# Norm factors by a full matrix of ones in seven root-mean-square norms of a two-stack transformer kernel

## The chip, the cores and the metric

The kernel runs on one core of one Trainium2 chip. The metric is the device time of one execution in microseconds (us), the median of several runs. The engines are named as the profile names them: PE (TensorE matmul), PEld (its weight loads), DVE (VectorE), ACT (ScalarE), POOL (GpSimd), SP (the queue that issues the DMAs).

## The reference

Two stacks of two layers each over 512 positions (and 256 context positions in the first layer) with 1024 channels: attention and a Fourier mix, gated linear attention and mLSTM style mixers, sliding attention, and feed-forward blocks. What matters here is the norm that stands ahead of nearly every block:

```python
def rms_norm(x, g):
    xf = x.astype(jnp.float32)
    y = xf * lax.rsqrt(jnp.mean(xf * xf, axis=-1, keepdims=True) + NORM_EPS)
    return (y * g.astype(jnp.float32)).astype(x.dtype)
```

The mean runs over the 1024 channels of one position, and one factor per position then scales all its channels.

## The kernel before, in words

Activations lie transposed: channels on the 128 partitions, positions along the free axis, so that x is KT = 8 tiles of 128 x n, with n = 768 (512 positions and 256 of context) in the first layer and n = 512 later. Every projection is `linear` (L393 is its matmul line): PE takes a unit of 128 x 1024 weights, split by ACT (L340, WHI) and DVE (L349, WLO) into two parts, and does three passes of each tile against a high and a low part of the activations. Those two parts are made by the norm ahead of the projection.

A norm needs sums over partitions. Class `Squares` gathers them: as each output tile of the projection before it is ready, ACT squares it (`square`, L533), tile 0 straight into RS and the others into one of two SQ buffers, and DVE adds tiles 1 to 6 to RS (`add`, L543). The last tile, 7, stays in SQ. Then `root` (L622) runs the steps below, each waiting for the one before it:

- PE, `Squares.sums` (L545 to L558): for each piece t of 128 positions, a matmul with 128 columns of RS as the stationary side and one column of ones as the moving side (L553), and the same for SQ (L556); the sums of 128 positions come out as one column of 128 partitions in bank 7. That is n/128 pairs: 4, or 6 for n = 768.
- ACT: square root of these 4 or 6 columns, into RC (L652); the mean's scale and the epsilon go in as scale and bias.
- DVE: reciprocal of 4 or 6 columns (L662).
- PE: spread (L640): one matmul per 128 positions with the broadcast column as stationary side and the identity as moving side, so that bank 6 (and 7 for n = 768) holds the factor of each position on every partition.
- DVE then scales: `normalize` (L700), `final_norm` (L2739) or `add_normed` (L2783), one `scalar_tensor_tensor` per tile, x times gain times the factor, which it reads from PSUM (`root_of`, L666). ACT makes the high part (L691, L689, L2808), DVE the low part (L715, L713, L2791), and PE starts the next `linear` when tile 0 of both is there. In the norms with a modulation, DVE makes the gains of both conditions between the reciprocal and the first scaling (`prep`, L731, two small operations).

While these steps run, no other work is queued on PE, so that it stands still outside L553, L556 and L640. `Squares` with this `root` is used in seven norms, here numbered by their place: norm 1 (first stack, layer 0, ahead of the feed-forward, n = 768), norm 2 (layer 1, ahead of the mixer, n = 768), norm 3 (layer 1, ahead of the feed-forward), norm 4 (`final_norm` of the first stack), norm 5 (second stack, `add_normed` behind the first mixer), norm 6 (`normalize` ahead of the second mixer), norm 7 (`add_normed` behind the second mixer), the last five with n = 512. Four other calls of `root` don't take the changed way: two use `LateSquares` (sums by PE tile by tile, L585), and two carry a `mean` (L649, L659). `TileNorm` (L974 to L996) has its own copy of the old steps.

The order of all work is the order of the code on each engine; ring buffers and semaphores (`mark`, `wait_ge`) tie the engines together.

Of the kernel before, what the change touches and what calls it, by code (L numbers as in the profile page):

```python
# [512 lines left out]
class Squares:  # L513


    def __init__(self, c, nk, n, size):
        self.c, self.nk, self.n, self.size = c, nk, n, size
        self.squared = c.mark("act", nk)
        self.added = c.mark("dve", nk - 2)
        self.summed = c.mark("pe")  # L520

    def place(self, k):
        return self.c.sq(k, self.n) if k else self.c.RS[:, 0:self.n]
# [21 lines left out]
    def sums(self, pe):  # L545

        c = self.c
        for token in c.bank_free.get(7, ()):
            pe.wait_ge(*token)
        pe.wait_ge(*self.added.at(self.nk - 2))  # L550
        for t in range(self.n // P):
            out = c.bank(7, 1, NC + t)
            pe.matmul(out, c.RS[:, t * P:(t + 1) * P], c.ONES[:, 0:1], start=True, stop=False)  # L553
            if t == 0:
                pe.wait_ge(*self.squared.at(self.nk))
            mm = pe.matmul(out, self.place(self.nk - 1)[:, t * P:(t + 1) * P], c.ONES[:, 0:1], start=False, stop=True)  # L556
        mm.then_inc(*self.summed.up())
        return self.summed.at(1)  # L558


class LateSquares:


    def __init__(self, c, nk, n, size):
        self.c, self.nk, self.n, self.size = c, nk, n, size
        self.squared = c.mark("act", nk)
        self.added = c.mark("pe", nk)
        self.given = 0

    def square(self, act, k, source, ready, bias=None):  # L570
        act.wait_ge(*ready)
# [50 lines left out]
def root(c, squares, over, mean=None):  # L622


    sqrt, rec, spread = c.mark("act"), c.mark("dve"), c.mark("pe")
    floored = c.mark("dve") if mean is not None else None
    n = squares.n
    nt = n // P
    summed = []
    block = c.stage()  # L630

    @block.tensor
    def _(pe):
        summed.append(squares.sums(pe))
        for token in c.bank_free.get(6, ()):
            pe.wait_ge(*token)
        pe.wait_ge(*rec.at(1))
        for t in range(nt):
            out = c.bank(6, P, t * P) if t < 4 else c.bank(7, P, (t - 4) * P)
            mm = pe.matmul(out, c.RC[:, 8 + t:9 + t].broadcast_to([P, P]), c.ID[:], start=True, stop=True)  # L640
        mm.then_inc(*spread.up())
        c.bank_free[6] = [over]
        c.bank_free[7] = [over] if nt > 4 else [sqrt.at(1)]

    @block.scalar
    def _(act):
        if mean is not None:
            act.wait_ge(*floored.at(1))
            act.activation(c.RC[:, 0:nt], c.RC[:, 0:nt], ACT.Sqrt).then_inc(*sqrt.up())  # L649
            return  # L650
        act.wait_ge(*summed[0])
        act.activation(c.RC[:, 0:nt], c.bank(7, nt, NC), ACT.Sqrt, bias=c.EPSC[:, 0:1], scale=1.0 / squares.size).then_inc(*sqrt.up())  # L652

    @block.vector
    def _(dve):
        if mean is not None:
            dve.wait_ge(*mean.taken.at(2))
            dve.wait_ge(*summed[0])
            dve.scalar_tensor_tensor(c.RC[:, 0:nt], c.bank(7, nt, NC), 1.0 / squares.size, c.RC[:, 4:4 + nt], ALU.mult,  # L659
                                     ALU.add).then_inc(*floored.up())  # L660
        dve.wait_ge(*sqrt.at(1))
        dve.reciprocal(c.RC[:, 8:8 + nt], c.RC[:, 0:nt]).then_inc(*rec.up())  # L662
    return spread


def root_of(c, lo, n):  # L666

    return c.bank(6, n) if lo == 0 else c.bank(7, n)


def normalize(c, squares, gain, xp, shift=None, keep=None, prep=None):


    n, nk = squares.n, squares.nk
    parts = conds(n)
    scaled, hi, lo = c.mark("dve", nk), c.mark("act", nk), c.mark("dve", nk)
    xh, xl, xw = xp
    spread = root(c, squares, scaled.at(nk))
    block = c.stage()
    place = keep or (lambda k, a, m: c.ht(k % 3, a, m))  # L680

    @block.scalar
    def _(act):
        for k in range(nk):
            act.wait_ge(*scaled.at(k + 1))
            for q, a, m in parts:
                o = xh[:, k * xw + a:k * xw + a + m]
                if shift is None:
                    ins = act.activation(o, place(k, a, m), ACT.Copy)  # L689
                else:  # L690
                    ins = act.activation(o, place(k, a, m), ACT.Identity, bias=shift(k, q))  # L691
            ins.then_inc(*hi.up())

    @block.vector
    def _(dve):
        def scale(k):
            if k >= 3:
                dve.wait_ge(*lo.at(k - 2))
            for q, a, m in parts:
                ins = dve.scalar_tensor_tensor(place(k, a, m), c.x(k, a, m), gain(k, q), root_of(c, a, m), ALU.mult, ALU.mult)  # L700
            ins.then_inc(*scaled.up())
        if prep is not None:
            prep(dve)
        dve.wait_ge(*spread.at(1))
        scale(0)
        for k in range(nk):
            if k + 1 < nk:
                scale(k + 1)
            dve.wait_ge(*hi.at(k + 1))
            for q, a, m in parts:  # L710
                o = slice(k * xw + a, k * xw + a + m)
                if shift is None:
                    ins = dve.tensor_tensor(xl[:, o], place(k, a, m), xh[:, o].bitcast(F32), ALU.subtract)  # L713
                else:
                    ins = dve.scalar_tensor_tensor(xl[:, o], place(k, a, m), shift(k, q), xh[:, o].bitcast(F32), ALU.add, ALU.subtract)  # L715
            ins.then_inc(*lo.up())
    return lambda k: lo.at(k + 1)
# [231 lines left out]
class TileNorm:  # L949
# [50 lines left out]
    def apply(self, dve):  # L1000
        dve.wait_ge(*self.spread.at(1))
        for k in range(self.nk):
            for q, a, m in conds(self.n):
                x = self.tiles_of[k](a, m)
                ins = dve.scalar_tensor_tensor(x, x, self.gain(k), root_of(self.c, a, m), ALU.mult, ALU.mult)
            ins.then_inc(*self.done.up())


# [1718 lines left out]
def final_norm(c, squares, late):  # L2727


    scaled = c.mark("dve", KT)  # L2730
    spread = root(c, squares, scaled.at(KT))
    block = c.stage()
    out = lambda k: c.H[:, k * NL:(k + 1) * NL]

    @block.vector
    def _(dve):
        dve.wait_ge(*spread.at(1))
        for k in range(KT):
            dve.scalar_tensor_tensor(out(k), c.x(k), c.vec("g_final", k), root_of(c, 0, NL), ALU.mult, ALU.mult).then_inc(*scaled.up())  # L2739

    @block.scalar
    def _(act):
        for k in range(KT):
            late.square(act, k, out(k), scaled.at(k + 1))
    c.X, c.H, c.stride = c.H, c.X, NL
    return scaled.at(KT)
# [24 lines left out]
def add_normed(c, squares, gain, dst, xp, mean=None, up=None):  # L2771


    scaled, added = c.mark("dve", KT), c.mark("dve", KT)
    hi, lo = c.mark("act", KT), c.mark("dve", KT)
    spread = root(c, squares, scaled.at(KT), mean)
    block = c.stage()
    xh, xl, xw = xp

    @block.vector  # L2780
    def _(dve):
        def scale(k):
            dve.scalar_tensor_tensor(dst(k), dst(k), c.vec(gain, k), root_of(c, 0, NL), ALU.mult, ALU.mult).then_inc(*scaled.up())  # L2783

        def low(k):
            dve.wait_ge(*hi.at(k + 1))
            q = slice(k * xw, k * xw + NL)
            if up is None:
                ins = dve.tensor_tensor(xl[:, q], c.x(k), xh[:, q].bitcast(F32), ALU.subtract)
            else:  # L2790
                ins = dve.scalar_tensor_tensor(xl[:, q], c.x(k), c.vec(up, k), xh[:, q].bitcast(F32), ALU.mult, ALU.subtract)  # L2791
            ins.then_inc(*lo.up())
        dve.wait_ge(*spread.at(1))
        scale(0)
        for k in range(KT):
            if k + 1 < KT:
                scale(k + 1)
            dve.wait_ge(*scaled.at(k + 1))
            dve.tensor_tensor(c.x(k), c.x(k), dst(k), ALU.add).then_inc(*added.up())  # L2799
            if k:  # L2800
                low(k - 1)
        low(KT - 1)

    @block.scalar
    def _(act):
        for k in range(KT):
            act.wait_ge(*added.at(k + 1))
            act.activation(xh[:, k * xw:k * xw + NL], c.x(k), ACT.Copy,  # L2808
                           scale=1.0 if up is None else c.vec(up, k)).then_inc(*hi.up())
    return lambda k: lo.at(k + 1)  # L2810
# [268 lines left out]
```

## Time and profile before

| | |
|---|---|
| median of 3 runs | 3479.46 us (3477.65 to 3481.04) |
| profiled execution, its own time | 3470.54 us |
| its span, first to last instruction | 3468.8 us |
| mean granted TensorE clock | 0.957 of full |
| PE busy | 3229.4 us, 93% |
| PEld busy | 2542.6 us, 73% |
| DVE busy | 1550.0 us, 45% |
| ACT busy | 1167.3 us, 34% |
| POOL busy | 193.2 us, 6% |
| `linear` matmuls, L393 | 2049.6 us (x7200) and 1245.7 us (x3600) |

Busy times are those of the profiled execution, and shares are of its span. The granted clock is the share of full speed (2.4 GHz) that PE was given; 0.50 is 1.2 GHz. Matmuls are pipelined, and their ends are modelled. The f32 matmuls of a norm stand in the trace as two records each ("x16" are eight matmuls). The number in brackets behind a timeline row is how long the engine sat idle before it, and what ended that.

### The profile page before, as it was taken

The page shows a single profiled execution, that of the slowest core. Times are in us where ns is not written, and L with a number is a line of the kernel's source. Part 1 is how long each engine was busy: PE and PEld are TensorE (multiplying, and loading weights), DVE is VectorE, ACT ScalarE, POOL GpSimd, SP SyncE. Part 2 cuts the span into 40 slices and gives each one's busy share as a digit, 9 for nine tenths or more (in the row PEclk, how much of TensorE's full clock was granted, in tenths as well). Part 3 has the DMA queues.
Part 4 walks back from the last instruction along what each step waited for, and adds up shares of the span by engine and source line. Part 5 has one row for each costly group of instructions (what it writes and reads, how often), then busy time and mean ns, then how long its engine had stood idle before and what let it go on. Part 6 is the DMA issues. An engine that isn't in the chain of part 4 may idle for free.

```text
span 3468.8 us, 42192 instructions
## 1 busy us (share of the span) xinstructions
PE 3229.4 (93%) x17354; PEld 2542.6 (73%) x17354; DVE 1550.0 (45%) x2331; ACT 1167.3 (34%) x1892; POOL 193.2 (6%) x222
## 2 busy tenths in 40 slices
PE   7898899999999899999998899999999887899998
PEld 5655587887888656778887677878888665688886
DVE  2145535434445345464555453254444455354444
ACT  3134433313223234343334532233223333332232
POOL 0012200000000012100000010000000024100000
PEclk9899999999999899999998899899999888899998
DMA  6500013333112200122222101122222110122221
GB/s 242 211 18 1 1 49 143 112 117 139 61 61 90 82 10 1 49 85 97 97 91 72 53 32 43 37 79 103 93 96 97 59 49 25 67 98 92 97 97 55
DMA packets 74030, 269.26 MB, mean 78 GB/s; under 512 B 9064, under 2 KB 9832, under 8 KB 72560
## 3 DMA queue, kind: packets, MB, share of 16 engines
q1 hardware_dynamic: 73840, 266.57, 21.8%
q8 instruction: 139, 2.28, 0.3%
q14 instruction: 51, 0.42, 0.0%
HBM read 264.44 MB, written 2.10 MB: 77 GB/s over the span
## 4 chain that ended last, share of the span: by engine, by line
PE 83%; DVE 8%; ACT 3%; issue 3%; DMA 2%; POOL 1%; SPq 0%; POOLq 0%; ACTq 0%; DVEq 0%
PE PS L393 62%; PE PS L1285 2%; PE PS L1262 2%; PE PS L1188 2%; PE PS L480 2%; DVE room L1468 1%; PE PS L1272 1%; POOL room L2582 1%; PE PS L585 1%; PE PS L1242 1%; DMA RING<-in_stream 1%; PE PS L640 1%; DMA room<-in_w_ada 1%; PE PS L2905 1%; DVE H L2799 1%
## 5 line engine op out<-in xcount | busy, mean ns | idle before, releaser
L393 PE MATMUL PS<-room,WHI 128*128 128x512 f32 (+1 forms) x7200 | 2049.6, 381 | 54.9 <-DVE room L715 13.8
L393 PEld LDWEIGHTS PS<-room,WHI 128*128 128x128 f32 x7200 | 1275.7, 191 | 353.6 <-issue 98.8
L393 PE MATMUL PS<-room,WLO 128*128 128x512 f32 (+1 forms) x3600 | 1245.7, 376 | 0.0
L393 PEld LDWEIGHTS PS<-room,WLO 128*128 128x128 f32 x3600 | 640.5, 191 | 128.8
L349 DVE TENSOR_TENSOR WLO<-RING,WHI 128x1024 fp32r<-128x1024 f32 x371 | 453.6, 1223 | 383.9 <-ACT WHI L340 382.9
L340 ACT ACTIVATE WHI<-RING 128x1024 fp32r<-128x1024 f32 x371 | 390.1, 1054 | 545.7 <-PE PS L393 534.4
L831 DVE SCALAR_TENSOR_TENSOR H<-PS,VEC,H 128x511 f32<-128x511 f32 (+1 forms) x132 | 83.1, 657 | 307.4 <-ACT H L809 307.4
L809 ACT ACTIVATE H<-PS,VEC 128x512 f32<-128x512 f32 (+1 forms) x132 | 88.4, 703 | 349.0 <-PE PS L393 349.0
L1262 PE MATMUL PS<-room 96*128 96x256 f32 (+1 forms) x432 | 154.3, 476 | 11.2 <-ACT SQ L1373 7.7
L774 DVE SCALAR_TENSOR_TENSOR X<-PS,MOD,X 128x512 f32<-128x512 f32 x96 | 60.5, 658 | 221.4 <-PE PS L393 221.3
L1468 DVE TENSOR_REDUCE room<-PS 128x1 f32<-128x768 f32 (+1 forms) x120 | 101.8, 849 | 100.8 <-PE PS L1262 100.3
L1262 PEld LDWEIGHTS PS<-room 96*128 96x128 f32 x432 | 73.8, 190 | 64.9 <-issue 51.2
L2847 DVE TENSOR_TENSOR room<-PS,room 128x512 f32<-128x512 f32 x64 | 44.2, 690 | 169.8 <-ACT room L2843 113.8
L1488 POOL TENSOR_SCALAR room<-room 128x768 f32<-128x768 f32 (+1 forms) x60 | 49.2, 821 | 1197.4 <-DVE room L1454 1197.4
L2843 ACT ACTIVATE room<-PS 128x512 f32<-128x512 f32 x64 | 38.2, 596 | 204.5 <-PE PS L393 204.5
L1285 PE MATMUL PS<-room 128*64 128x128 f32 x1248 | 81.4, 277 | 25.1 <-ACT room L1345 21.0
L1285 PEld LDWEIGHTS PS<-room 128*64 128x64 f32 x1248 | 67.2, 137 | 47.5 <-ACT room L1345 44.8
L1448 DVE COPY room<-PS 128x384 f32<-128x384 f32 (+1 forms) x120 | 59.4, 495 | 86.6 <-PE PS L1272 86.6
L2871 DVE TENSOR_TENSOR X<-X,PS 128x512 f32<-128x512 f32 x48 | 32.9, 686 | 135.4 <-PE PS L393 135.4
L836 DVE SCALAR_TENSOR_TENSOR H<-PS,VEC,H 128x511 f32<-128x511 f32 (+1 forms) x132 | 83.2, 658 | 3.1
L1188 PE MATMUL PS<-room 128*128 128x512 f32 (+1 forms) x210 | 77.8, 517 | 1.5 <-ACT SQ L1373 1.3
L1373 ACT ACTIVATE SQ<-PS,room 128x768 f32<-128x768 f32 (+1 forms) x60 | 48.9, 815 | 82.4 <-DVE room L1468 82.4
(354 smaller groups left out, 2706.8 us busy)
## 6 DMA issues: line engine op xcount, KB each, us to landing
RING<-in_stream SPq DMA_DIRECT2D x370, 512.0 KB, 3.5
room<-in_w_ada SPq DMA_DIRECT2D x84, 512.0 KB, 5.7
H<-in_w_ada SPq DMA_DIRECT2D x12, 512.0 KB, 4.7
room<-in_consts SPq DMA_DIRECT2D x4, 1024.0 KB, 9.6
room<-in_wq SPq DMA_DIRECT2D x2, 1728.0 KB, 7.4
X<-in_x_in SPq DMA_DIRECT2D x2, 1536.0 KB, 10.6
room<-in_wple SPq DMA_DIRECT2D x2, 1024.0 KB, 4.9
out_dram<-H SPq DMA_DIRECT2D x8, 256.0 KB, 2.0
```

Of the source, the lines that this page charges most:

```text
L340: act.activation(c.WHI[:, w:w + UN], c.RING[:, r:r + UN], ACT.Copy).then_inc(c.w_hi, 1)
L349: dve.tensor_tensor(c.WLO[:, w:w + UN], c.RING[:, r:r + UN], c.WHI[:, w:w + UN].bitcast(F32), ALU.subtract).then_inc(c.w_lo, 1)
L393: mm = pe.matmul(acc, wt[:, w], xt[:, k * xw + lo:k * xw + lo + q], start=(k == 0 and z == 0), stop=(k == kt - 1 and z == 2))
L480: mm = pe.matmul(c.bank(self.bank, 512, 0, 32 * j, 32 * j + 32), c.SC[:, 32 * k:32 * k + 32], self.ring[self.slots[k]][j // 2][:, 512 * (j ...
L774: ins = dve.scalar_tensor_tensor(x, a, mod(c, self.l, self.part, j, q), x, ALU.mult, ALU.add)
L809: ins = act.activation(cv(i, z, lo, w), a, ACT.Identity, bias=col("b_dw", j), scale=col("dw1_", j))
L831: ins = dve.scalar_tensor_tensor(y, a[:, 0:w - 1], col("dw0_", j), y, ALU.mult, ALU.add)
L836: ins = dve.scalar_tensor_tensor(y, a[:, 1:w], col("dw2_", j), y, ALU.mult, ALU.add)
L1188: mm = pe.matmul(c.bank(b + r, m), c.a(w + k * stride, P), c.a(x + k * W + lo, m), start=(k == 0), stop=(k == kn - 1))
L1262: mm = pe.matmul(c.bank(b + r, m), q_at(p, z, i * P, P, 0, 96), k_at(p, z, k0 + lo, m, 0, 96), start=True, stop=True)
L1285: mm = pe.matmul(c.bank(6 + part, P, (i % 4) * P, 64 * z, 64 * z + 64), c.a(vv + (t0 + t) * 768 + (2 * pair + z) * 64, 64), turned_at(a + ...
L1468: dve.tensor_reduce(c.a(NEG + j, 1), c.PS[:, 512 * b:512 * b + n], AX, ALU.max, negate=True).then_inc(*neg.up())
```

## The change

`Squares` gets a field `total` (RS, n columns), and `root` hands over to a new `wide_root` where `total` is set and there is no `mean`. The squares' sums are taken with all of ONES, 128 x 128, as the stationary side and RS and then SQ as the moving side, 512 or 512 and 256 columns each, into bank 6 (and 7): every partition gets the sum of every position. ACT takes the square root of n columns from PSUM into RS, DVE the reciprocal of RS in place, and the scalings read RS instead of PSUM. L553, L556 and L640 are gone in these norms.

```diff
@@ Squares
-        self.summed = c.mark("pe")
+        self.summed = None
+        self.total = c.RS[:, 0:n]
@@ Squares.sums
+        self.summed = c.mark("pe")
@@ LateSquares
+        self.total = None
@@ root
+    if mean is None and squares.total is not None:
+        return wide_root(c, squares)
+    c.root_at = lambda lo, n: c.bank(6, n) if lo == 0 else c.bank(7, n)
@@
-def root_of(c, lo, n):
-
-    return c.bank(6, n) if lo == 0 else c.bank(7, n)
+def wide_root(c, squares):
+
+    spread, sqrt, rec = c.mark("pe"), c.mark("act"), c.mark("dve")
+    n = squares.n
+    root = c.RS[:, 0:n]
+    c.root_at = lambda lo, m: c.RS[:, lo:lo + m]
+    block = c.stage()
+
+    @block.tensor
+    def _(pe):
+        for b in (6, 7)[:len(conds(n))]:
+            for token in c.bank_free.get(b, ()):
+                pe.wait_ge(*token)
+            c.bank_free[b] = [sqrt.at(1)]
+        pe.wait_ge(*squares.added.at(squares.nk - 2))
+        for q, lo, m in conds(n):
+            pe.matmul(c.bank(6 + q, m), c.ONES[:], squares.total[:, lo:lo + m], start=True, stop=False)
+        pe.wait_ge(*squares.squared.at(squares.nk))
+        for q, lo, m in conds(n):
+            mm = pe.matmul(c.bank(6 + q, m), c.ONES[:], squares.place(squares.nk - 1)[:, lo:lo + m], start=False, stop=True)
+        mm.then_inc(*spread.up())
+
+    @block.scalar
+    def _(act):
+        act.wait_ge(*spread.at(1))
+        act.activation(root, c.PS[:, 6 * 512:6 * 512 + n], ACT.Sqrt, bias=c.EPSC[:, 0:1], scale=1.0 / squares.size).then_inc(*sqrt.up())
+
+    @block.vector
+    def _(dve):
+        dve.wait_ge(*sqrt.at(1))
+        dve.reciprocal(root, root).then_inc(*rec.up())
+    return rec
@@ normalize, and likewise final_norm and add_normed
     spread = root(c, squares, scaled.at(nk))
+    root_of = c.root_at
...
-                ins = dve.scalar_tensor_tensor(place(k, a, m), c.x(k, a, m), gain(k, q), root_of(c, a, m), ALU.mult, ALU.mult)
+                ins = dve.scalar_tensor_tensor(place(k, a, m), c.x(k, a, m), gain(k, q), root_of(a, m), ALU.mult, ALU.mult)
```

The first place is PE at norm 3, between the last matmul of one `linear` and the first of the next (UNCONDITIONAL_BRANCH is the step into the next stage). Before:

```order
L393 MATMUL PS<-room,WLO 128x512
L632 UNCONDITIONAL_BRANCH
L553 MATMUL PS<-ONES,RS 128x1
L556 MATMUL PS<-ONES,SQ 128x1
L553 MATMUL PS<-ONES,RS 128x1
...
L640 MATMUL PS<-ID,RC 128x128 x4
L378 UNCONDITIONAL_BRANCH
L393 MATMUL PS<-room,WHI 128x512 x2
```

And of the change:

```order
L393 MATMUL PS<-room,WLO 128x512
L681 UNCONDITIONAL_BRANCH
L689 MATMUL PS<-RS,ONES 128x512
L692 MATMUL PS<-SQ,ONES 128x512
L378 UNCONDITIONAL_BRANCH
L393 MATMUL PS<-room,WHI 128x512 x2
```

Eight matmuls of one column and four of 128 give way to two of 512 columns; nothing else of PE moves.

The second place is DVE at the same norm. Before:

```order
L543 TENSOR_TENSOR RS<-RS,SQ 128x512
L654 UNCONDITIONAL_BRANCH
L662 RECIPROCAL RC<-RC 128x4
L694 UNCONDITIONAL_BRANCH
L731 SCALAR_TENSOR_TENSOR AV<-MOD,VEC 128x8 x2
L700 SCALAR_TENSOR_TENSOR H<-X,AV,PS 128x512 x2
```

And of the change:

```order
L544 TENSOR_TENSOR RS<-RS,SQ 128x512
L700 UNCONDITIONAL_BRANCH
L703 RECIPROCAL RS<-RS 128x512
L731 UNCONDITIONAL_BRANCH
L768 SCALAR_TENSOR_TENSOR AV<-MOD,VEC 128x8 x2
L737 SCALAR_TENSOR_TENSOR H<-X,AV,RS 128x512 x2
```

The order is the same; the reciprocal is 512 columns wide instead of 4, and the scaling reads RS where it read PSUM.

## Rows read from the trace of the kernel before

**Rows 1.** The page, part 4: the chain that ended last, shares of the span.

```profile
PE 83%; DVE 8%; ACT 3%; issue 3%; DMA 2%; POOL 1%; SPq 0%; POOLq 0%; ACTq 0%; DVEq 0%
```

**Rows 2.** Timeline, norm 3: start us, us, engine, line, what [idle before <- releaser].

```profile
1468.51 0.40 PE L393 MATMUL PS<-room,WLO 128*128 128x512 f32 x1
...
1469.61 0.68 DVE L543 TENSOR_TENSOR RS<-RS,SQ 128x512 f32<-128x512 f32 x1
...
1470.44 0.35 PE L553 MATMUL PS<-ONES,RS 128*128 128x1 f32 x2 [1.53 <-DVE RS L543]
...
1473.27 0.26 ACT L652 ACTIVATE RC<-PS,EPSC 128x4 f32<-128x4 f32 x1 [2.87 <-PE PS L556]
1473.57 0.18 DVE L662 RECIPROCAL RC<-RC 128x4 f32<-128x4 f32 x1 [3.28 <-ACT RC L652]
1473.66 0.21 DVE L731 SCALAR_TENSOR_TENSOR AV<-MOD,VEC 128x8 f32<-128x8 f32 x2
1473.89 2.04 PE L640 MATMUL PS<-ID,RC 128*128 128x128 f32 x8 [0.66 <-DVE RC L662]
1476.06 1.41 DVE L700 SCALAR_TENSOR_TENSOR H<-X,AV,PS 128x512 f32<-128x512 f32 x2 [2.18 <-PE PS L640]
...
1477.59 0.75 DVE L715 SCALAR_TENSOR_TENSOR room<-H,MOD,room 128x512 fp32r<-128x512 f32 x1
```

**Rows 3.** Windows from first L553 to L652, norms 1 to 7: length, engines' busy times, clock.

```profile
517.03:520.58 3.55, 3.51 (x24) 3.42 (x24) 0.00 (x0) 0.00 (x1) 0.00 (x0) 0.77 0.00 0
1124.13:1127.24 3.11, 3.07 (x24) 2.99 (x24) 0.00 (x0) 0.00 (x0) 0.00 (x0) 0.88 0.96 353
1470.44:1473.27 2.83, 2.80 (x16) 2.71 (x16) 0.00 (x0) 0.00 (x0) 0.00 (x0) 0.65 0.00 0
1845.04:1847.09 2.05, 2.01 (x16) 1.92 (x16) 0.00 (x0) 0.01 (x1) 0.00 (x0) 0.91 0.00 0
2320.04:2323.11 3.07, 2.92 (x16) 2.74 (x16) 0.00 (x0) 0.42 (x1) 0.00 (x0) 0.69 0.87 315
2765.34:2768.92 3.58, 3.54 (x16) 3.45 (x16) 0.00 (x0) 1.21 (x2) 0.00 (x0) 0.50 0.09 37
3021.04:3023.36 2.32, 2.07 (x16) 1.90 (x16) 0.00 (x0) 0.51 (x1) 0.00 (x0) 1.00 0.91 293
```

**Rows 4.** Timeline, a 512-column f32 matmul pair of the gated embedding, full clock.

```profile
3418.33 1.88 PE L2905 MATMUL PS<-room 128*128 128x512 f32 x4
```

**Rows 5.** Groups of ACT by form: what, out<-in | busy us, mean ns of one.

```profile
L2759 ACT ACTIVATE room<-PS,VEC 128x512 f32<-128x512 f32 x8 | 5.5, 687 | 26.6 <-PE PS L393 26.6
L652 ACT ACTIVATE RC<-PS,EPSC 128x6 f32<-128x6 f32 x3 | 0.8, 267 | 6.8 <-PE PS L556 6.8
```

**Rows 6.** Groups of DVE by form: every width of reciprocal in the kernel.

```profile
L1454 DVE RECIPROCAL room<-room 128x1 f32<-128x1 f32 x120 | 18.4, 154 | 0.8 <-ACT SQ L1373 0.4
L662 DVE RECIPROCAL RC<-RC 128x4 f32<-128x4 f32 x8 | 1.4, 178 | 26.9 <-ACT RC L652 26.4 <-ACT RC L649 0.5
L662 DVE RECIPROCAL RC<-RC 128x6 f32<-128x6 f32 x3 | 0.6, 191 | 7.6 <-ACT RC L652 7.6
L2156 DVE RECIPROCAL room<-room 128x16 f32<-128x16 f32 x1 | 0.2, 247 | 0.0
```

**Rows 7.** Groups of DVE by form: scalings that read PSUM (L700), one that doesn't (L715).

```profile
L715 DVE SCALAR_TENSOR_TENSOR room<-H,MOD,room 128x512 fp32r<-128x512 f32 x24 | 17.9, 746 | 1.1
L700 DVE SCALAR_TENSOR_TENSOR H<-X,AV,PS 128x512 f32<-128x512 f32 x24 | 17.7, 741 | 11.2 <-PE PS L640 11.2
...
L700 DVE SCALAR_TENSOR_TENSOR H<-X,AV,PS 128x256 f32<-128x256 f32 x18 | 8.5, 472 | 0.0
```

**Rows 8.** Windows from end of gains or reciprocal to first scaling, norms 1, 5, 7, then all seven's sum.

```profile
521.18:524.23 3.05, 2.90 (x12) 2.64 (x12) 0.00 (x1) 0.00 (x0) 0.00 (x0) 0.50 0.00 0
...
2323.59:2325.82 2.23, 2.04 (x8) 1.78 (x8) 0.00 (x1) 0.00 (x0) 0.00 (x0) 0.50 0.46 187
...
3023.84:3025.76 1.92, 1.74 (x8) 1.47 (x8) 0.01 (x1) 0.00 (x0) 0.00 (x0) 0.63 0.88 363
sum 16.90, PE 15.72 PEld 13.85 DVE 0.03 ACT 0.00 POOL 0.00; mean PE 2.25 PEld 1.98 DVE 0.00 ACT 0.00 POOL 0.00
```

**Rows 9.** Windows of PE behind norms 2 and 3, from the first L393: length, PE busy, clock.

```profile
1134.52:1143.00 8.48, 8.48 (x33) 0.67 0.01 2
1478.49:1487.00 8.51, 8.51 (x31) 0.82 0.01 2
```

More of the change, by code:

```diff
@@ L1004, in apply @@
                 x = self.tiles_of[k](a, m)
-                ins = dve.scalar_tensor_tensor(x, x, self.gain(k), root_of(self.c, a, m), ALU.mult, ALU.mult)
+                ins = dve.scalar_tensor_tensor(x, x, self.gain(k), self.c.bank(6 if a == 0 else 7, m), ALU.mult, ALU.mult)
             ins.then_inc(*self.done.up())
@@ L2731, in final_norm @@
     spread = root(c, squares, scaled.at(KT))
+    root_of = c.root_at
     block = c.stage()
@@ L2738, in _ @@
         for k in range(KT):
-            dve.scalar_tensor_tensor(out(k), c.x(k), c.vec("g_final", k), root_of(c, 0, NL), ALU.mult, ALU.mult).then_inc(*scaled.up())
+            dve.scalar_tensor_tensor(out(k), c.x(k), c.vec("g_final", k), root_of(0, NL), ALU.mult, ALU.mult).then_inc(*scaled.up())
     @block.scalar
@@ L2776, in add_normed @@
     spread = root(c, squares, scaled.at(KT), mean)
+    root_of = c.root_at
     block = c.stage()
@@ L2782, in scale @@
         def scale(k):
-            dve.scalar_tensor_tensor(dst(k), dst(k), c.vec(gain, k), root_of(c, 0, NL), ALU.mult, ALU.mult).then_inc(*scaled.up())
+            dve.scalar_tensor_tensor(dst(k), dst(k), c.vec(gain, k), root_of(0, NL), ALU.mult, ALU.mult).then_inc(*scaled.up())
         def low(k):
```

## The prediction

> **What bounds the kernel now.** I read the chain of waits first: PE holds 83% of it and DVE 8% [rows 1], so most of the time is the stream of L393 matmuls, which the change leaves alone. What the change touches lies in the gaps of that stream, so I then read the timeline of one norm [rows 2]. PE's last matmul starts at 1468.51, DVE adds the last but one square until 1470.29, PE takes the column sums from 1470.44, ACT starts its root at 1473.27, DVE its reciprocal at 1473.57, PE spreads from 1473.89, and the first scaling starts at 1476.06. Each step is released by the one before, and the timeline shows PE with nothing but the norm's own matmuls between. The same pattern stands at all seven norms. So whatever a step of this chain gains or loses, the end of the kernel gains or loses: no term below has a cover. The last thing I read is what the clock does there, since PE works part of the time at half speed: in the sums the granted clock averages 0.50 to 1.00 [rows 3].
>
> **The change, part by part.** All sums are over norms 1 and 2 (768 columns) and norms 3 to 7 (512).
>
> *Column sums.* Before, from the first L553 to the start of the root: 3.55, 3.11, 2.83, 2.05, 3.07, 3.58 and 2.32 us, in all 20.51 [rows 3]. After, two f32 matmuls of 512 columns: four records that take 1.88 us at full clock in the nearest row [rows 4]. Of this about 0.17 is the drain behind the last column, an estimate that leaves 0.43 for each record; so 1.71 us of work for 512 columns, 2.57 for 768, and about 0.21 for drain and hand-over to ACT (the 0.17 and 0.04 of semaphore). The clock: if it falls where it fell before, the stretch at full clock is length times (2 x clock - 1), thus 1.92, 2.36, 0.85, 1.68, 1.17, 0 and all [rows 3], and what is left of the work takes twice its time. That gives 3.43, 2.99, 2.78, 1.95, 2.46, 3.63 and 1.92, in all 19.2: **-1.3 us**. The bounds: full clock everywhere but in norm 6, which began at 0.50, gives 2 x 2.78 + 4 x 1.92 + 3.63 = 16.9, -3.6; half clock everywhere gives 2 x 5.35 + 5 x 3.63 = 28.9, +8.3. I take -1.3, since the idle time ahead of the sums, after which the clock fell, is unchanged.
>
> *Root.* ACT's root of 4 columns took 0.26 [rows 2], of 6 columns 267 ns [rows 5]. For 512 columns from PSUM with a bias the nearest row is 687 ns [rows 5]; from that pair, 0.83 ns a column, so 768 columns come to 0.90. 5 x 0.42 + 2 x 0.63 = **+3.4 us**. The bounds are near: the function is another, not the width.
>
> *Reciprocal.* This decides. The trace holds widths of 1, 4, 6 and 16 columns only: 154, 178, 191 and 247 ns [rows 6]. An ordinary DVE operation costs (741 - 472)/256 = 1.05 ns a column [rows 7]; the reciprocal costs (247 - 154)/15 = 6.2 ns from 1 to 16. A line of 146 ns and 6.25 ns a column gives 152, 171, 184 and 246, close to all four. I extend it: 3.35 us for 512 columns and 4.95 for 768, and the difference is 5 x (3.35 - 0.18) + 2 x (4.95 - 0.19) = **+25.4 us**. The bounds: the flattest piece among the rows (6 to 16) has 5.6 ns and gives 3.02 and 4.46, +22.7; the steepest (1 to 4) has 8.0 ns and gives 4.24 and 6.29, +32.5; and if the slope were a thing of short rows and the rest went at 1.05, 0.69 and 0.96, +4.1. I take the line through all four, as the sixteen-column row is the nearest and lies on it.
> The Trainium skill (VectorE: DVE Perf Modes, Walkthrough: the 8-slice pipeline in each mode) says that the reciprocal runs divide steps "with a repeat count of 8". At 1.05 ns a step that would be 8.4 ns a column, 4.45 and 6.60 us, and this term +34.2 instead of +25.4. The trace disagrees at its widths: by 8.4 ns the 16 columns would take 154 + 15 x 8.4 = 280 ns, and they took 247.
>
> *Spread.* L640 is gone. Before, DVE sat idle behind reciprocal and gains for 16.90 us over the seven norms, from 3.05 each in norms 1 and 2 to 1.92 in norm 7 [rows 8]; all of it goes: **-16.9 us**. The gains (L731, 0.21 for the pair [rows 2]) stand between reciprocal and scaling as before, and cost what they did. In norms 4 to 7 the scaling now waits for the reciprocal on its own engine, about 0.03 each, **+0.1**.
>
> *Scaling.* The factor comes from SBUF instead of PSUM. The operation with PSUM takes 741 ns, and L715, the same kind with all operands outside PSUM, 746 [rows 7]. Zero; the bound is 5 ns for each first scaling, nothing.
>
> *What comes behind.* PE restarts the stream about 1.5 us later per norm, at half clock as now: the mean clock of the next 8.5 us was 0.67 behind norm 2 and 0.82 behind norm 3 [rows 9]. Twice (1 - clock) times length is the time at half speed, half of that is lost: 2.8 and 1.5 us, the extremes of six (norm 4 is followed by other work). Where the clock rises within the restart I can't tell, so zero, with about +-3 us over the six. RS stays in use until the last scaling; its next writer is a square of a later projection's output, behind the scaling anyway. Weight fetches and splits are done when the norm starts, and a longer gap does not delay them. Banks 6 and 7 are free sooner, and nobody waits for them.
>
> The sum: -1.3 + 3.4 + 25.4 - 16.9 + 0.1 = **+10.7 us**, about +1.2 for a norm of 512 columns and +2.4 for one of 768. Against the profiled execution that is a span of 3479.5 instead of 3468.8 and a time of 3481.2 instead of 3470.54. The median of the runs shown, 3479.46, lies 8.9 above the profiled one; I add to the median: **3490.2 us**. About 0.2%, 7 us, is what a measurement of this kernel can tell from no change.
>
> **The rivals.**
> 1. *The clock holds through the sums.* The wide matmuls stream 512 columns each where the old ones streamed one, and may keep the clock up in norms 1 to 5. For it: the fall came in the middle of the one-column matmuls in five norms [rows 3]. Against it: the idle time ahead is the same. Price: the -3.6 in place of -1.3, 3487.9 us.
> 2. *The reciprocal costs as in its steepest piece, 8.0 ns a column.* Then its term is +32.5 and the time 3497.3 us. Against it: the 16-column row. The page named above would put it at 8.4 ns a column, 3499.0 us.
> 3. *The other side: a wide reciprocal streams at one column per step.* The slope of the short rows would be filling, and 512 columns would take 0.69 us, less than the spread that is removed. The term is +4.1, the sum -10.6, the time 3468.9 us. The point from which it decides: without the reciprocal's term the sum is -14.7, and seven wide reciprocals have 4096 columns together, so the change is faster if a column costs under about 3.6 ns. Against it: from 6 to 16 columns the cost still rises by 5.6 ns each, with no flattening.
> 4. *It is not all on the path*, or it reaches fewer norms (the change speaks of six; the instruction order shows seven wide reciprocals). Six would be +9.5; a cover of some microseconds, or a lucky restart, brings it within 0.2% of before: 3483 us.
>
> **How the numbers follow.** The forecast as summed 0.58, rival 1 0.22, rival 2 0.07, rival 3 0.05, rival 4 0.08. The likeliest case by itself runs from 3484.5 (flattest reciprocal, -2.7, and a lucky clock, -3) to 3495. To leave out no more than 2 in 10, the range is 3484 to 3498; it holds rivals 1 and 2 at their rows' prices and leaves out rivals 3 and 4. Slower by over 0.2% needs 3486.4: the forecast and rivals 1 and 2, less the low ends of the first two: 0.83. Within 0.2%: rival 4 and those low ends, 0.12. Faster: rival 3, 0.05.
>
> **What would show it.** In the new profile: L703 as a group of five at 3.35 us and two at 4.95; L698 at 0.69 and 0.90; L689 and L692 together under 2 us in norm 7 and near 3.6 in norm 6; the scaling L737 still 741 ns; no L640 but four times; in norm 3 PE idle for about 6.7 us between L692 and the next L393 (0.69 + 3.35 + 0.2 for root, reciprocal and gains, and the 2.4 from the first scaling to L393 as now [rows 2, 9]). Wrong would be: a reciprocal under 2.0 us for 512 columns, a scaling that is slower from RS, or a sum of the seven stretches from the first wide matmul to the first scaling that grows by far more or less than 10.7 us.

## The result, and the profile after

Over 20 runs of each, the changed kernel took 3486.15 us in the median (3471.07 to 3490.75), the kernel before 3474.8 (3466.16 to 3481.04): ratio 1.003, 95% interval 1.0021 to 1.0038, so about 10.4 us slower, between 7.3 and 13.2. The forecast was a change of +10.7. Its absolute 3490.2 lies 4 us high because it was added to the median of three runs, 3479.46, and 20 runs put the kernel before at 3474.8. The two medians by themselves differ by 11.35 us.

The profiled execution has a span of 3484.6 us, 15.8 more than before; its chain of waits, part 4 of the page, reads as before but for one line. The first row answers to [rows 1]; in the second, L703 stands where L640 stood, which is the reciprocal in place of the spread:

```profile
PE 83%; DVE 8%; ACT 3%; issue 3%; DMA 2%; POOL 1%; SPq 0%; POOLq 0%; ACTq 0%; DVEq 0%
PE PS L393 62%; PE PS L1322 2%; PE PS L1299 2%; PE PS L1225 2%; PE PS L480 2%; DVE room L1505 1%; PE PS L1309 1%; POOL room L2619 1%; PE PS L588 1%; PE PS L1279 1%; DMA RING<-in_stream 1%; DVE RS L703 1%; DMA room<-in_w_ada 1%; PE PS L2944 1%; DVE H L2838 1%
```

The timeline of norm 3 of the changed kernel, in the columns of [rows 2]:

```profile
1474.42 0.68 DVE L544 TENSOR_TENSOR RS<-RS,SQ 128x512 f32<-128x512 f32 x1
...
1475.25 1.10 PE L689 MATMUL PS<-RS,ONES 128*128 128x512 f32 x2 [1.53 <-DVE RS L544]
1476.18 1.02 PE L692 MATMUL PS<-SQ,ONES 128*128 128x512 f32 x2
1477.24 0.69 ACT L698 ACTIVATE RS<-PS,EPSC 128x512 f32<-128x512 f32 x1 [2.02 <-PE PS L692]
1477.96 3.35 DVE L703 RECIPROCAL RS<-RS 128x512 f32<-128x512 f32 x1 [2.86 <-ACT RS L698]
1481.23 0.17 DVE L768 SCALAR_TENSOR_TENSOR AV<-MOD,VEC 128x8 f32<-128x8 f32 x2
...
1483.88 1.19 PE L393 MATMUL PS<-room,WHI 128*128 128x512 f32 x2 [6.67 <-DVE room L752]
```

PE idles for 6.67 us ahead of L393, and 3.35 of it is one DVE instruction. The first scaling starts at 1481.44; from the first sum matmul to there is 6.2 us, against 5.6 in [rows 2].

The groups of the changed kernel that answer to [rows 5 to 7], DVE first:

```profile
L703 DVE RECIPROCAL RS<-RS 128x512 f32<-128x512 f32 x5 | 16.8, 3352 | 15.8 <-ACT RS L698 15.8
L737 DVE SCALAR_TENSOR_TENSOR H<-X,AV,RS 128x512 f32<-128x512 f32 x18 | 13.4, 747 | 0.1
L703 DVE RECIPROCAL RS<-RS 128x768 f32<-128x768 f32 x2 | 9.9, 4952 | 7.9 <-ACT RS L698 7.9
...
L737 DVE SCALAR_TENSOR_TENSOR H<-X,AV,PS 128x512 f32<-128x512 f32 x6 | 4.5, 744 | 2.7 <-PE PS L646 2.7
```

And those of ACT:

```profile
L698 ACT ACTIVATE RS<-PS,EPSC 128x512 f32<-128x512 f32 x5 | 3.4, 687 | 9.4 <-PE PS L692 9.4
L698 ACT ACTIVATE RS<-PS,EPSC 128x768 f32<-128x768 f32 x2 | 1.8, 900 | 5.9 <-PE PS L692 5.9
```

The windows from the first sum matmul to the root, norms 1 to 7, in the columns of [rows 3]:

```profile
517.74:520.60 2.86, 2.82 (x8) 1.41 (x8) 0.00 (x0) 0.00 (x1) 0.00 (x0) 1.00 0.00 0
1129.49:1132.34 2.85, 2.82 (x8) 1.41 (x8) 0.00 (x0) 0.00 (x0) 0.00 (x0) 1.00 0.96 374
1475.25:1477.24 1.99, 1.96 (x4) 0.65 (x4) 0.00 (x0) 0.00 (x0) 0.00 (x0) 1.00 0.00 0
1851.83:1853.82 1.99, 1.95 (x4) 0.65 (x4) 0.00 (x0) 0.00 (x0) 0.00 (x0) 1.00 0.00 0
2334.87:2336.86 1.99, 1.95 (x4) 0.65 (x4) 0.00 (x0) 0.42 (x1) 0.00 (x0) 1.00 0.83 259
2780.45:2784.00 3.55, 3.50 (x4) 1.15 (x4) 0.00 (x0) 1.22 (x2) 0.00 (x0) 0.56 0.11 44
3036.34:3038.34 2.00, 1.96 (x4) 0.65 (x4) 0.00 (x0) 0.52 (x2) 0.00 (x0) 1.00 0.87 242
```

In norms 1 to 5 the clock stays at 1.00, where it averaged 0.65 to 0.91 before [rows 3].

To compare the profiles, each norm is cut at four points of its timeline: first sum matmul, root, first scaling, next L393. (Behind norm 4 the next L393 comes only after another norm, of the `LateSquares` kind, so that its third stretch is 20.4 us long and makes half of that column.) The sums over the seven norms, in us (the last column is the span less the fourth):

| kernel | sums | root to first scaling | first scaling to L393 | all | rest of the span |
|---|---|---|---|---|---|
| before | 20.5 | 20.6 | 40.5 | 81.6 | 3387.2 |
| changed | 17.2 | 32.6 | 40.5 | 90.4 | 3394.2 |
| e1_twice | 19.9 | 58.3 | 40.5 | 118.7 | 3394.3 |
| e2_narrow | 17.2 | 7.3 | 38.7 | 63.2 | 3399.2 |
| e3_lnexp | 17.2 | 19.7 | 40.5 | 77.4 | 3386.5 |
| e4_fill | 18.8 | 32.6 | 40.5 | 92.0 | 3385.7 |
| e5_old_warm | 17.2 | 18.1 | 40.6 | 75.8 | 3387.2 |
| e6_lnexp_warm | 15.7 | 19.7 | 39.6 | 75.1 | 3383.1 |
| e7_again | 16.3 | 32.7 | 40.5 | 89.5 | 3394.4 |
| e8_old_pre | 16.1 | 17.8 | 40.5 | 74.4 | 3381.9 |

So of the 15.8 us between the two profiled spans 8.8 are made in the norms, and 7.0 outside. Part of the 7.0 is the choice of executions: the profiled one of the kernel before (3470.54) was 4.3 us faster than its median, that of the changed kernel (3486.43) lay at its median. What is known of the remainder stands in the last section.

### The profile page after: what moved, and what is told of

Read it like the earlier page. It is cut to its first block, busy times and chain, and to the rows that moved or that the text cites. A ratio compares the mean times of both kernels' runs of the same rounds, so it can differ in the third digit from the quotient of the medians.

```text
span 3484.6 us, 41873 instructions
## 1 busy us (share of the span) xinstructions
PE 3215.5 (92%) x17198; PEld 2519.7 (72%) x17198; DVE 1575.8 (45%) x2331; ACT 1170.9 (34%) x1892; POOL 193.2 (6%) x222
## 4 chain that ended last, share of the span: by engine, by line
PE 83%; DVE 8%; ACT 3%; issue 3%; DMA 2%; POOL 1%; SPq 0%; POOLq 0%; ACTq 0%; DVEq 0%
PE PS L393 62%; PE PS L1322 2%; PE PS L1299 2%; PE PS L1225 2%; PE PS L480 2%; DVE room L1505 1%; PE PS L1309 1%; POOL room L2619 1%; PE PS L588 1%; PE PS L1279 1%; DMA RING<-in_stream 1%; DVE RS L703 1%; DMA room<-in_w_ada 1%; PE PS L2944 1%; DVE H L2838 1%
## 5 line engine op out<-in xcount | busy, mean ns | idle before, releaser
L393 PE MATMUL PS<-room,WHI 128*128 128x512 f32 (+1 forms) x7200 | 2052.7, 382 | 84.2 <-DVE room L752 29.8
L393 PEld LDWEIGHTS PS<-room,WHI 128*128 128x128 f32 x7200 | 1275.7, 192 | 385.9 <-issue 129.7
L393 PE MATMUL PS<-room,WLO 128*128 128x512 f32 (+1 forms) x3600 | 1246.4, 376 | 0.0
L393 PEld LDWEIGHTS PS<-room,WLO 128*128 128x128 f32 x3600 | 641.9, 191 | 128.3
L480 PE MATMUL PS<-room,SC 128*32 128x512 f32 x336 | 61.1, 755 | 18.8 <-DMA room<-in_w_ada 18.8
```

The costliest lines, as they stand in the source:

```text
L393: mm = pe.matmul(acc, wt[:, w], xt[:, k * xw + lo:k * xw + lo + q], start=(k == 0 and z == 0), stop=(k == kt - 1 and z == 2))
L480: mm = pe.matmul(c.bank(self.bank, 512, 0, 32 * j, 32 * j + 32), c.SC[:, 32 * k:32 * k + 32], self.ring[self.slots[k]][j // 2][:, 512 * (j ...
```

## The experiments

The questions were: is the reciprocal alone the loss, and on the path in full; what do the clock's states in the sums and at the restart cost; and can the norm be made cheaper than both kernels have it.

**e1_twice: the reciprocal a second time.**

```diff
+        dve.reciprocal(c.sq(0, n), root)
         dve.reciprocal(root, root).then_inc(*rec.up())
```

> The changed kernel with a second reciprocal of the same width in each of the seven norms (its output goes to an unused buffer and is not read). Theory (the reciprocal lies wholly on the path, 3.35 us for 512 columns and 4.95 for 768): 5 x 3.35 + 2 x 4.95 = 26.7 us more than the changed kernel, about 37 us more than before, ratio near 1.0107. Rival (part of the gap has a cover, or the clock gives time back when the gap is longer): less than 20 us more than the changed kernel.

3507.5 us against 3471.51 for the kernel before on the same chips, ratio 1.0104 (1.0078 to 1.0129): 36 us over the kernel before. The norms took 118.7 us, 28.4 more than in the changed kernel. Its groups of DVE:

```profile
L703 DVE RECIPROCAL SQ<-RS 128x512 f32<-128x512 f32 x5 | 16.8, 3353 | 15.2 <-ACT RS L698 15.2
L704 DVE RECIPROCAL RS<-RS 128x512 f32<-128x512 f32 x5 | 16.5, 3295 | 0.0
L703 DVE RECIPROCAL SQ<-RS 128x768 f32<-128x768 f32 x2 | 9.9, 4953 | 11.2 <-ACT RS L698 11.2
L704 DVE RECIPROCAL RS<-RS 128x768 f32<-128x768 f32 x2 | 9.8, 4895 | 0.0
```

16.5 + 9.8 = 26.3 us were added, and the root-to-scaling column grew by 25.7, so all but 0.6 of it shows as path time. The other 2.7 are the sums: the clock fell within those of norms 1 and 2 in this execution (4.55 and 4.46 us instead of 2.86 and 2.85, 3.3 more), and norm 6's took 0.6 less. The rival, a cover, falls.

**e2_narrow: the reciprocal over 4 or 6 columns, the rest as in the change.** It leaves out the true factor.

```diff
-        act.activation(root, c.PS[:, 6 * 512:6 * 512 + n], ACT.Sqrt, bias=c.EPSC[:, 0:1], scale=1.0 / squares.size)...
+        act.activation(root, c.PS[:, 6 * 512:6 * 512 + n], ACT.Sqrt, bias=c.ONES[:, 0:1], scale=0.0)...
...
-        dve.reciprocal(root, root).then_inc(*rec.up())
+        dve.reciprocal(c.RS[:, 0:n // P], c.RS[:, 0:n // P]).then_inc(*rec.up())
```

> The changed kernel with the reciprocal over the first 4 (or 6) columns only; the root is taken of a constant, so that this kernel leaves out the inverse and the true factor, all else being as in the change. Theory (the reciprocal's columns are the whole loss): 25.2 us less than the changed kernel, about 15 us less than before, ratio near 0.9957. Rival (something else holds the restart, as weights or a bank): a gain of under 15 us over the changed kernel, so no faster than before.

Ratio to before 0.9972 (0.9956 to 0.9988), some 10 us faster than before, where 15 was expected; 15 is at the edge of the interval. The groups of the reciprocal, to be set against 3352 and 4952 ns:

```profile
L703 DVE RECIPROCAL RS<-RS 128x4 f32<-128x4 f32 x5 | 0.9, 178 | 15.8 <-ACT RS L698 15.8
L703 DVE RECIPROCAL RS<-RS 128x6 f32<-128x6 f32 x2 | 0.4, 192 | 7.9 <-ACT RS L698 7.9
```

In the norms the loss and more is gone: root to scaling 7.3 instead of 32.6, which is 25.3, and 25.2 was expected. The first scaling still leads to L393 in 3.63 us in norms 1 and 2 and 2.44 in norm 3, so nothing else holds the restart. The norms are 18.4 us shorter than before; 1.9 of that lie behind the first scaling of norm 4, where the 64 one-column matmuls of the next norm (L588) took 11.90 us at a clock of 0.59 against 13.79 at 0.50 before (L585). The time did not follow in full. In the profile the rest of the span is the longest of all ten, 3399.2, and it isn't one odd execution: the median of 12 runs lies 9.2 us below the kernel before, and even the edge of the interval, 15, is less than 18.4. Something outside the norms takes back several us in this kernel; what, isn't shown.

**e3_lnexp: the inverse root by ACT, as exp(-0.5 ln v), no reciprocal.**

```diff
-            act.activation(self.c.RC[:, 15:16], self.c.EPSC[:, 0:1], ACT.Sqrt)
+            act.activation(self.c.RC[:, 15:16], self.c.EPSC[:, 0:1], ACT.Ln)
...
-        act.activation(root, ..., ACT.Sqrt, bias=c.EPSC[:, 0:1], scale=1.0 / squares.size)...
-        dve.reciprocal(root, root)...
+        act.activation(root, ..., ACT.Ln, bias=c.EPSC[:, 0:1], scale=1.0 / squares.size)...
+        act.wait_ge(*sqrt.at(1))
+        act.activation(root, root, ACT.Exp, scale=-0.5)...
```

(The first pair is the one-column operation ahead of the squares that has ACT's function table in place before the root.)

> The changed kernel with the factor as exp(-0.5 ln(mean + eps)): both steps by ACT over all columns, no reciprocal. Removed: 5 x 3.38 + 2 x 4.98 = 26.9 us of DVE. Added by ACT: seven table loads of 1.28 between the two steps, 5 x 0.63 + 2 x 0.84 for the second step, 13.8 us. Theory: 13 us less than the changed kernel, 2 to 3 less than before, ratio 0.999. Rival (more table loads later in the stages eat it): no better than the changed kernel.

Ratio 1.0002 (0.9987 to 1.0018): the loss of the change is gone, a gain over the kernel before isn't shown. The norms took 77.4 us, 13.0 less than in the changed kernel, as worked out. ACT's groups:

```profile
L700 ACT ACT_TABLE_LOAD x7 | 9.0, 1283 | 0.1
L698 ACT ACTIVATE RS<-PS,EPSC 128x512 f32<-128x512 f32 x5 | 3.4, 687 | 9.4 <-PE PS L692 9.4
L700 ACT ACTIVATE RS<-RS 128x512 f32<-128x512 f32 x5 | 3.1, 629 | 0.1
```

Root and inverse by ACT with a table load between take 2.66 us from root to first scaling for 512 columns (norms 4 to 7), where root and DVE's reciprocal take 4.11. The kernel as a whole has 57 table loads, the kernel before and the changed one 44. Whether the six table loads that it adds elsewhere cost the difference between -4 in the norms and the +1 measured was not tried apart.

**e4_fill: matmuls of no use while DVE inverts.** A helper, called behind the wide sums (`c.post` gives the count for each norm):

```diff
+def busy(c, pe, count, bank=7):
+    for _ in range(count):
+        pe.matmul(c.bank(bank), c.ONES[:], c.VEC[:, 0:512], start=True, stop=True)
...
         mm.then_inc(*spread.up())
+        busy(c, pe, next(c.post), spare)
```

> The changed kernel with matmuls of no use (ones by a constant table, 512 columns, into a free bank) behind the wide sums of six norms: 10, 10, 7, 0, 9, 5, 9 of them, 0.86 us each at full clock, so that PE is busy nearly until the next L393. Theory (PE's idle gap is what makes the clock low at the restart, and the low clock there costs half its length wherever PE and not DVE sets the pace): full clock from the first L393, and a gain of 2.0 + 1.6 + 3.0 + 1.7 = 8 us in norms 1, 2, 3 and 6, none in norms 5 and 7, where DVE needs 1.93 us for each tile and PE 1.37: ratio to before about 1.0007. Rival (the clock is low whatever PE did, or the matmuls delay the restart): ratio 1.003 or more.

Ratio 1.0018 (1.0001 to 1.0034), 4 us below the changed kernel's 1.003, where 8 were expected. The intervals overlap (the changed kernel's goes from 1.0021 to 1.0038), so the times by themselves don't show a gain. The windows of 8 us from the first L393 behind norms 1, 2, 3, 5, 6 and 7, in the columns of [rows 9]; first the changed kernel:

```profile
530.23:538.23 8.00, 8.00 (x35) 0.75 0.01 2
1141.98:1149.98 8.00, 8.00 (x37) 0.80 0.00 0
1483.88:1491.88 8.00, 8.00 (x23) 0.62 0.00 0
2345.06:2353.06 8.00, 8.00 (x25) 0.69 0.00 0
2790.39:2798.39 8.00, 8.00 (x28) 0.79 0.01 2
3046.53:3054.53 8.00, 7.73 (x26) 0.79 0.00 0
```

Then e4_fill:

```profile
530.60:538.60 8.00, 8.00 (x45) 1.00 0.01 2
1141.35:1149.35 8.00, 8.00 (x45) 1.00 0.01 2
1483.68:1491.68 8.00, 8.00 (x35) 1.00 0.01 2
2337.75:2345.75 8.00, 6.98 (x26) 1.00 0.01 2
2782.63:2790.63 8.00, 8.00 (x28) 0.79 0.00 0
3039.57:3047.57 8.00, 6.96 (x26) 1.00 0.01 2
```

The clock is at 1.00 from the first L393 in five of six (norm 6 got the fewest matmuls, and its sums began at half clock). Behind norms 1 to 3, PE gets through 45, 45 and 35 records where it had 35, 37 and 23. Behind norms 5 and 7 it gets through 26, where it had 25 and 26 at 0.69 and 0.79, and is idle for a microsecond, each time waiting for the low part that DVE makes: there DVE's three operations per tile set the pace. From the restart to ACT's first read of a finished output the times say the same: 17.96, 17.44 and 13.39 us in the changed kernel, 16.18, 16.17 and 10.58 in e4_fill, together 5.9 less; and 13.3 us behind norms 5 and 7 in both. So the low clock at the restart costs 1 to 3 us where PE sets the pace, and nothing where DVE does. (The same kernel moves by up to 0.9 us there, with its clock: e7_again, the changed kernel again, has 18.80, 17.67 and 13.37.) Norm 6 gave nothing, and norm 2's sums happened to run partly at half clock (4.54 us).

**e5_old_warm: the same in the kernel before.** Column sums, narrow root and spread stay; PE's idle time ahead of the sums and behind the spread is filled.

```diff
...
+            busy(c, pe, next(c.pre), spare)
         summed.append(squares.sums(pe))
...
...
         mm.then_inc(*spread.up())
...
+            busy(c, pe, next(c.post), spare)
```

> The kernel before (column sums, narrow root and reciprocal, spread) with 512-column matmuls of no use in PE's idle time of the seven norms: 2, 2, 1, 1, 1, 3, 1 ahead of the sums, while PE waits for the last add, and 4, 4, 2, 0, 4, 2, 4 behind the spread. Theory (wide matmuls hold the clock, and the low clock is paid in sums, spread and restart): sums 16 us instead of 20.5, spread 7 us less, restart 9 us less in norms 1, 2, 3 and 6; about 20 us less than before, ratio 0.9942. Rival (one-column and 128-column matmuls lose the clock whatever ran ahead of them, so that only little is won): ratio 0.998 or more.

3457.95 us against 3471.14 for the kernel before, ratio 0.9968 (0.9954 to 0.9982): 11 us faster than the kernel before (13 between the medians), little more than half of what was expected. The clock at the restart came out (0.96 or more in all six), its worth only in part: 6.0 us less to ACT's first reads in norms 1, 2 and 3, 0.1 in norm 6 and nothing in norms 5 and 7, where 9 were expected. The sums took 17.2 instead of 16, as the clock fell within those of norm 1 (3.83 us at 0.71) and norm 4 (0.91) in spite of the matmuls ahead. The spread missed by most: root to scaling shrank by 2.5 us where 7 were expected. In norms 1, 2, 4 and 7 the clock had fallen by the time of the spread.

**e8_old_pre: only the matmuls ahead of the sums.**

> The kernel before with only the idle matmuls ahead of the column sums (2, 2, 1, 1, 1, 3, 1), none behind the spread. Theory (wide matmuls hold the clock for a while, also through the one-column matmuls behind them): sums near 16 us instead of 20.5 and part of the spread's 7 us, the restart as before: 5 to 10 us less than before, ratio 0.9975 to 0.9985. Rival (the clock falls in the sums all the same): the sums near 20 us, ratio 1.000.

Ratio 0.998 (0.9967 to 0.9993), 7 us faster than before, as expected. Norm 3 in its timeline, against [rows 2]:

```profile
1463.07 1.02 PE L626 MATMUL PS<-VEC,ONES 128*128 128x512 f32 x2
...
1464.77 0.35 PE L554 MATMUL PS<-ONES,RS 128*128 128x1 f32 x2 [0.68 <-DVE RS L544]
...
1466.72 0.26 ACT L667 ACTIVATE RC<-PS,EPSC 128x4 f32<-128x4 f32 x1 [1.99 <-PE PS L557]
...
1467.34 1.13 PE L653 MATMUL PS<-ID,RC 128*128 128x128 f32 x8 [0.66 <-DVE RC L677]
1468.59 1.41 DVE L715 SCALAR_TENSOR_TENSOR H<-X,AV,PS 128x512 f32<-128x512 f32 x2 [1.26 <-PE PS L653]
```

One 512-column matmul in the idle 1.5 us ahead of the sums keeps the clock through the same column matmuls (1.95 us instead of 2.83) and here through the spread too (1.13 instead of 2.04), as in norms 5 and 6; in norms 1, 2 and 7 the spread gained nothing and in norm 4 next to nothing. Over the seven norms the sums take 16.1 us, and root to scaling 17.8 instead of 20.6; the norms end 7.2 us shorter. The matmuls ahead do two things at once: they are wide, and they shorten PE's idle time ahead of the sums, from 0.88 to 2.89 us to 0.02 to 0.68. Which of the two keeps the clock in the old kernel was not tried apart.

**e6_lnexp_warm: e3_lnexp with the idle matmuls ahead and behind.**

> The kernel with exp(-0.5 ln(mean + eps)) by ACT (no reciprocal) and the same kind of idle matmuls: 2, 2, 1, 1, 1, 3, 1 ahead of the wide sums and 7, 7, 5, 0, 7, 4, 7 behind them. Theory: 4 us less than before in the norms as without them, 1.6 less in norm 6's sums, 8 to 9 less at the restarts: 13 to 15 us less than before, ratio 0.996. Rival (the further table loads of the second step eat it): ratio 0.999 or more.

3459.92 us, ratio 0.9963 (0.9948 to 0.9979), 13 us faster than before, as expected. It is not told apart from e5_old_warm; both beat the kernel before and the changed one.

**e7_again: the change itself beside these.**

> The changed kernel itself, unedited, beside the others of this call on the same chip. The norms' stretches as in its first trace (from the first wide matmul to the next L393 90.4 us in all, give or take 2 for the clock in the sums), ratio to before 1.003.

Ratio 1.0028 (1.0012 to 1.0044), norms 89.5 us. The change's cost repeats, in the time and in the norms.

## Why the prediction was right

*The path.* Right: e1_twice shows reciprocal time to be path time (25.7 us of 26.3), e2_narrow takes it off the norms again. PE's idle time ahead of L393 in norm 3, 6.67 us, was forecast as 6.7.

*The reciprocal.* Right to the digits: 3352 and 4952 ns against 3.35 and 4.95. The line through widths 1, 4, 6 and 16 [rows 6] carries to 768 columns. Rival 2 (8.0 ns a column) and rival 3 (1.05 ns) fall with it. So does the estimate from the Trainium skill (VectorE: DVE Perf Modes, Walkthrough: the 8-slice pipeline in each mode), whose repeat count of 8 read as eight steps a column gives 4.45 and 6.60 us: the measured slope, (4952 - 3352)/256 = 6.25 ns, is six times the 1.05 of [rows 7].

*The root.* 687 and 900 ns against 0.69 and 0.90. *The spread* gone, *the scaling* unmoved (747 from RS, 744 from PSUM). Together with the reciprocal these terms were +12.0 us, and root to first scaling went from 20.6 to 32.6.

*The column sums.* This is the term that was mis-sized. I took -1.3, with the clock falling where it fell before; the profile shows 17.2 instead of 20.5, -3.3, close to rival 1's -3.6, and e7_again 16.3. The step that failed is "since the idle time ahead of the sums, after which the clock fell, is unchanged". That idle time is indeed unchanged (2.19, 2.19, 1.53, 1.53 and 0.88 us ahead of norms 1 to 5 in both kernels), and yet the clock fell in all five in the one profile of the kernel before, and in none in the changed kernel. So the clock depends on what PE streams just then as well: 512-column matmuls keep it where one-column matmuls let it fall. It is not certain either: six profiles have the wide sums with nothing put ahead of them, and of their 30 norms numbered 1 to 5 three had the clock fall within the sums (e1_twice norms 1 and 2, e4_fill norm 2).

*What comes behind.* Taken as zero with +-3 us. In this pair the restarts were worth 0.35 and 1.27 less in norms 1 and 2 and 1.4 more in norm 3 (0.5 more, 1.0 less and 1.4 more in e7_again), so zero was fair. I had counted a loss of half the low time for six norms; e4_fill shows that it is none behind norms 5 and 7.

With rival 1's sums the norms grew by 8.8 us (7.9 in e7_again), and the measured ratio says 10.4, 7.3 to 13.2. Both the forecast's 10.7 and rival 1's 8.4 lie in it, so the time alone can't choose between them; the windows of the sums do, for rival 1. That the forecast came within 0.3 us of the measured change is thus partly luck: it had the norms 2 us too long, and what brings the time back to 10.4, if that is taken at its word, came from outside the norms, where it had put zero.

*A slip in the sum.* By its own terms a norm of 768 columns was to grow by 2.2 us, not 2.4; the total is not touched. The two grew by 1.7 and 2.1.

*Six norms or seven.* Seven reciprocals stand in the profile.

## What to carry to other kernels

DVE's reciprocal costs per column six times what an ordinary operation does (6.25 against 1.05 ns), so it belongs where the data is narrowest: inverting 4 columns and spreading them by matmul (4 columns 0.18 us, spread 2.2) beats inverting 512 equal copies (3.35 us). Read the price of a wide operation from every narrow width that the trace has: four rows gave it within a per cent. In a chain of short steps between matmul streams, look at the granted clock step by step, and put wide matmuls of no use into PE's idle time there; it took 11 us (ratio 0.9954 to 0.9982) off this kernel (e5_old_warm). About half came within the norms, where e8_old_pre shows it alone (7 us), and half at the restart, where it pays only if PE and not DVE sets the pace.

## What the runs showed of the hardware

- One to three idle 512-column f32 matmuls in the wait ahead of a burst of one-column matmuls kept the clock at 0.96 to 1.00 through the burst in all seven norms of e8_old_pre (16.1 us of sums against 20.5). It is not sure: the same matmuls ahead in e5_old_warm kept it in five of seven (0.71 in norm 1, 0.91 in norm 4).
- The share of the span outside the norms moved between 3381.9 and 3399.2 us; its work is the same but for the table loads of e3_lnexp and e6_lnexp_warm and the clock at the restarts. Most of the difference between these two is the stretch between norms 4 and 5, from the next L393 to the sums of norm 5: the mixer of small chained matmuls. Its window in e2_narrow and then in e8_old_pre (length, busy times, clock):

```profile
1857.53:2319.52 461.99, 439.41 (x3225) 354.81 (x3225) 189.74 (x357) 166.59 (x279) 17.73 (x24) 0.91 0.14 48
```

```profile
1863.37:2310.77 447.40, 425.16 (x3227) 343.38 (x3227) 189.73 (x357) 166.47 (x279) 17.74 (x24) 0.94 0.15 49
```

DVE, ACT and POOL are busy for the same time to 0.2 us, PE for 14 us more at a clock of 0.91 than at 0.94. The kernel before had 449.9 us at 0.93, the changed one 456.6 at 0.92, which is 6.7 of the 7.0 us that the two profiles differ by outside the norms. It doesn't account for every long rest: in e1_twice, with 3394.3, this stretch took 450.5.

- One and the same kernel moves with the clock from one execution to the next: the 29 runs of the kernel before that were taken beside e1_twice go from 3456.92 us at a mean granted clock of 0.962 to 3484.67 at 0.954. So two profiled spans can differ by 10 us and more with nothing changed, and only stretches cut at the same instructions can be compared.

- Whether the changed kernel's longer stretch between norms 4 and 5 is such a chance or comes of the change stays open. It took 456.6 us in the changed kernel, 456.7 in e7_again and 462.0 in e2_narrow, and 447.4 to 452.3 in the other seven profiles, which speaks for the change; but e1_twice, which has the change too, is among the seven. Why the clock is granted otherwise there stays open as well.
